# First weight unit of an MLP split ahead of its stage, in buffers of its own

## The chip, the core and the metric

One NeuronCore of a Trainium2 chip runs the whole kernel in one launch. The core has TensorE (matrix multiplication; matmul and weight load are told apart), VectorE, ScalarE, GpSimd and SyncE; the last issues DMAs and waits. The metric is the device time of one execution in microseconds (us). Before the change it was 2215.55 us, the median of 3 runs (2215.15 to 2217.57).

## The reference

One encoder block on `x` (512 frames of 2048 values, float32) with a conditioning vector `c`:

```python
mod = (c_act @ w_ada[i] + b_ada[i])[:, None, :]
shift_m, scale_m, gate_m, shift_f, scale_f, gate_f = jnp.split(mod, N_MOD, axis=-1)

h = rmsnorm(x, g_pre_mix[i]) * (1.0 + scale_m) + shift_m
y = token_mixer(h, w_in[i], ..., w_out[i])          # attention and linear attention, output projection
x = x + gate_m * rmsnorm(y, g_post_mix[i])

h = rmsnorm(x, g_pre_mlp[i]) * (1.0 + scale_f) + shift_f
y = squared_relu_mlp(h, w_mlp_in[i], w_mlp_out[i])  # hidden width 8192
x = x + gate_f * rmsnorm(y, g_post_mlp[i])
```

The change lies between the end of `@ w_out` and the first columns of `h @ w_mlp_in`.

## The kernel before

**Split matmuls.** Each float32 operand is kept as two numbers, a rounded high part and the rest as a low part. One product is three matmuls: high by high, low by high and high by low (`split_mm`, lines 804 to 806). Weights arrive in raw form by DMA, ScalarE copies them to the high part (`split_hi`, line 1246), and VectorE subtracts that from the raw weights for the low part (`split_lo`, line 1716).

**Weight units.** The output projection and the first MLP read their weights in units of 1 MB (512 rows by 512 columns). There are two raw buffers (`w_raw`), two for the high part (`w_hi`) and two for the low part (`w_lo`), all 8 KB per partition, and unit m uses number m % 2 of each. SyncE loads a unit when the one two before it has been split (`slot_free`, line 520). Both splits of a unit wait until TensorE has used the unit two before it (`w_used`, which counts used units). In the program's count the output projection's units are M_OUT to M_OUT + 15; those of the first MLP start at M_MLP.

**The seam.** The output projection runs in four groups of 512 columns. Behind its last group each row block t of 128 frames is squared and summed (`square_y`), multiplied by its gain (`gain_y`), scaled by a root that GpSimd computes (`y_root`) and added to the residual (`add_y`, for rows 2 and 3 in two halves). The sum is squared again (`square_x1`, row 3 in halves), GpSimd computes the next root (`x1_root`), and `scale_x1` gives the normed rows, which TensorE transposes (`x1_transpose`, line 1080). The transposed tile is modulated, rounded to its high part on ScalarE (`modulated_hi`, line 1548) and its low part is made on VectorE (`piece_lo`, line 2212).

**Pieces.** The first MLP block (512 hidden columns) begins before rows 2 and 3 are ready. Its input is cut into 24 pieces:

```python
PIECES = [(slice(h * HALF, (h + 1) * HALF), k) for h in range(2) for k in range(KT // 2)]
PIECES += [(slice(0, SEQ), k) for k in range(KT // 2, KT)]
```

Pieces 0 to 7 are frames 0 to 255 of the inner tiles k = 0 to 7, pieces 8 to 15 frames 256 to 511 of the same tiles, pieces 16 to 23 all frames of k = 8 to 15. Unit 0 holds the weights of k = 0 to 3, so pieces 0 to 3 and 8 to 11 read it; unit 1 serves pieces 4 to 7 and 12 to 15, unit 2 pieces 16 to 19, unit 3 pieces 20 to 23. Unit 0 counts as used at the end of piece 11. A piece has twelve matmuls (four column tiles of 128, three each), with transpositions for a later piece behind it.

**Orders.** Each engine's order is written out by hand. ScalarE: after the projection's last squares and two squares of x1, the split of unit 0, then pieces with squares between; unit 1 is split between pieces 2 and 3, unit 2 behind piece 13's rounding, unit 3 behind piece 17's. VectorE has the matching order. ScalarE multiplies the first gate load by `c` behind the roundings of pieces 19 and 21. SyncE loads units 0, 1 and 2 of the first MLP, then issues the loads for a row of the second gate (`load_gate`, line 618: two of 1 MB into the buffers `ada0`, line 598, and two rows, lines 621 and 623), then loads unit 3 and the next block's units. The buffers `ada0` lie in a region of 16 KB per partition (`R_AD`) that also holds the items of the first gate (`ag_item`), read for the last time in the projection's second group, and, in the second MLP, two raw buffers.

The program ends on a chain through TensorE; the second MLP follows the first without a pause.

Of the kernel before, what the change touches and what calls it, by code (L numbers as in the profile page):

```python
# [45 lines left out]
def build_block(nc, x, c, w_ada, b_ada, g_pre_mix, g_post_mix, w_in, b_fgate, w_gla_a2, b_gla_a2,  # L46
# [67 lines left out]
    with ExitStack() as ctx:  # L114
# [27 lines left out]
        o_junk = at("o_junk", [P, 4, 512], R_A + 8 * KIB)  # L142
        y_t1 = at("y_t1", [P, 2, 4, 512], R_A + 16 * KIB)
        y_t2 = at("y_t2", [P, 2, 4, 512], R_A + 32 * KIB)
        RAW2_AT = (R_C + 32 * KIB, R_C + 40 * KIB, R_AD, R_AD + 8 * KIB, R_A + 56 * KIB)
        v_raw = [at(f"v_raw{s}", [P, 2, 1024], RAW2_AT[s]) for s in range(5)]
        v_op = [at(f"v_op{s}", [P, 2, 1024], R_C + 8 * KIB * s, F32R) for s in range(4)]
        w_raw = [at(f"w_raw{s}", [P, 2048], R_C + 8 * KIB * s) for s in range(2)]
        w_hi = [at(f"w_hi{s}", [P, 2048], R_C + 8 * KIB * (2 + s), F32R) for s in range(2)]
        w_lo = [at(f"w_lo{s}", [P, 2048], R_C + 8 * KIB * (4 + s), F32R) for s in range(2)]  # L150
        grp = at("grp", [P, TILES, SEQ], R_G)
        y = at("y", [P, TB, D], R_G)

# [243 lines left out]

        def arrived_out(cg, mm):
            return RAW_OUT + 16 * (cg * (MM_O // 2) + mm // 2 + 1)

        def arrived_mlp(b, mm):
            return RAW_MLP + 16 * (b * (MM_O // 2) + mm // 2 + 1)
# [116 lines left out]
        def _(sp):  # L519
# [203 lines left out]
            for b in range(FBS):  # L723
                for mm in range(MM_O):
                    load_m1(b, mm)
                    if b % 2 == 0 and mm == 2:
                        load_gate(Q_GF + b // 2, b // 2, GATE_F, g_post_mlp)
                    if b and mm == MM_O - 1 and b - 1 < FBS - 2:
                        store_hidden(b - 1)
# [71 lines left out]
        def _(pe):  # L801
# [331 lines left out]

            def first_mlp_in():
                for n, (cols, k) in enumerate(PIECES):
                    s, m = (k // 4) % 2, M_MLP + k // 4
                    hi, lo = wide_view(w_hi[s])[:, k % 4, :], wide_view(w_lo[s])[:, k % 4, :]
                    if k % 4 == 0:
                        pe.wait_ge(hi_done, m + 1)
                        pe.wait_ge(lo_done, m + 1)  # L1140
                    pe.wait_ge(mod_lo, KT + n + 1)
                    for t in range(4):
                        last = split_mm(bank[t][:, cols], (hi[:, t * P:t * P + P], lo[:, t * P:t * P + P]),
                                        (in_hi[:, k, cols], in_lo[:, k, cols]), k == 0 and n == 0, n == SECOND - 1 or k == KT - 1,
                                        onto=n >= SECOND)
                        if k == KT - 1 and t < 3:
                            last.then_inc(h_sum, 1)
                        if n >= SECOND and t == 3 and k % 4 == 3:
                            last.then_inc(w_used, 1)
                    for following in TRANSPOSES_AT.get(n, ()):  # L1150
                        x1_transpose(following)

            def mlp_in(b):
                steps = [(k, t) for k in range(KT) for t in range(4)]
                if b == LAST:
                    steps = steps[:12 * 4] + [(k, t) for t in range(4) for k in range(12, KT)]
                for k, t in steps:
                    s, m = (k // 4) % 2, M_MLP + b * MM_O + k // 4
                    hi, lo = wide_view(w_hi[s])[:, k % 4, :], wide_view(w_lo[s])[:, k % 4, :]
                    if t == 0 and k % 4 == 0:  # L1160
                        pe.wait_ge(hi_done, m + 1)
                        pe.wait_ge(lo_done, m + 1)
                    if k == 0:
                        if b >= 2:
                            pe.wait_ge(h_relu, 4 * (b - 2) + t + 1)
                        if b == 1:
                            pe.wait_ge(mod_tmp, KT + N_PIECES)
                        if b and b % 2 == 0 and t == 3:
                            pe.wait_ge(ada_col, Q_GF + b // 2)
                    last = split_mm(bank[4 * (b % 2) + t][:, :], (hi[:, t * P:t * P + P], lo[:, t * P:t * P + P]),  # L1170
                                    (in_hi[:, k, :], in_lo[:, k, :]), k == 0, k == KT - 1)
                    if k == KT - 1 and t < 3:
                        last.then_inc(h_sum, 1)
                    if t == 3 and k % 4 == 3:
                        last.then_inc(w_used, 1)
                    if b % 2 and k == KT - 2 and t == 0 and b < LAST or b == LAST and k == KT - 5 and t == 0:

                        pe.wait_ge(h_relu, 4 * b)
                        ada_rows(Q_GF + b // 2, bank[3])
# [61 lines left out]
        def _(act):  # L1241
            def split_hi(m, arrived, n, view=whole_view):
# [2 lines left out]
                act.wait_ge(w_used, m - 1)  # L1245
                act.activation(view(w_hi[n]), view(w_raw[n]), ACT.Copy).then_inc(hi_done, 1)  # L1246


            def next_hi_group(r, mm, last, view):

# [277 lines left out]
            for cg in range(CG):  # L1528
                if cg:
                    for mm in range(2, MM_O):  # L1530
                        split_hi_out(cg * MM_O + mm)
                if cg < CG - 1:
                    split_hi_out(cg * MM_O + MM_O)
                    for t in range(TB):
                        square_y(cg, t)
                    split_hi_out(cg * MM_O + MM_O + 1)
# [18 lines left out]
            square_y(CG - 1, 1)  # L1555
            square_x1(0, 1)
            square_x1(1, 2)
            split_hi_out(CG * MM_O)
            square_y(CG - 1, 2)
            first_piece(0)  # L1560
            square_y(CG - 1, TB - 1)
            first_piece(1)
            first_piece(2)
            split_hi_out(CG * MM_O + 1)
            first_piece(3)
            first_piece(4)
            square_x1(2, 4)
# [7 lines left out]
            for n in range(SECOND, N_PIECES):  # L1575
                if n == N_SECOND:
                    modulate_first(n)
                modulated_hi(n)
                if n in (13, 17):
                    split_hi_out(CG * MM_O + (n - 5) // 4)  # L1580
                if n in (19, 21):
                    ada_times_c(Q_GF, n // 21)
            act.wait_ge(x1_out, 16 * TB)

            def hidden(b):
# [11 lines left out]
                    if b == LAST:  # L1597
                        square_hidden(b, t)
                if b < LAST:
                    split_hi(M_MLP + b * MM_O + 5, arrived_mlp(b + 1, 1), 1)  # L1600
                    for t in range(4):
                        square_hidden(b, t)
                act.wait_ge(h_sq, 4 * b + 4)
# [15 lines left out]
            for b in range(FBS):  # L1619
                for mm in range(MM_O if b == 0 else 0, MM_O):  # L1620
                    if mm != 1:
                        split_hi(M_MLP + b * MM_O + mm, arrived_mlp(b, mm), mm % 2)
                    if mm == 0:
                        hidden(b - 1)
                    if b % 2 == 0 and mm >= 2:
                        ada_times_c(Q_GF + b // 2, mm - 2)
# [84 lines left out]
        def _(dve):  # L1711
            def split_lo(m, n, view=whole_view):
# [3 lines left out]
                dve.tensor_tensor(view(w_lo[n]), view(w_raw[n]), view(w_hi[n]).bitcast(F32), ALU.subtract)\  # L1716
                    .then_inc(lo_done, 1)


            def evict_fox(r, tiles):  # L1720
                for b in tiles:
# [459 lines left out]
            for cg in range(CG):  # L2181
                if cg:
                    for mm in range(2, MM_O):
                        split_lo(M_OUT + cg * MM_O + mm, mm % 2)
                        if cg == 1:
                            for i in (2 * mm - 4, 2 * mm - 3):
                                g_item(GLA_HEADS - 1, i, 0)
                                g_item(GLA_HEADS - 1, i, 1)
                if cg < CG - 1:
                    split_lo(M_OUT + cg * MM_O + MM_O, 0)  # L2190
                    if cg == 1:
# [28 lines left out]
                add_y(t, ALL)  # L2220
            scale_x1(0)
            scale_x1(1)
            split_lo(M_MLP, 0)
            piece_lo(0)
            total_y(2)
            gain_y(CG - 1, 2)
            piece_lo(1)
            total_y(TB - 1)
            gain_y(CG - 1, TB - 1)
            add_y(2, LEFT)  # L2230
            piece_lo(2)
            add_y(2, RIGHT)
            piece_lo(3)
            split_lo(M_MLP + 1, 1)
            piece_lo(4)
            add_y(TB - 1, LEFT)
            add_y(TB - 1, RIGHT)
            piece_lo(5)
            scale_x1(2)
            dve.wait_ge(x1_ss, TB + 1)  # L2240
            dve.tensor_reduce(ss_x[:, TB + 1:TB + 2], ss_x[:, TB - 1:TB + 1], AX_X, ALU.add).then_inc(x1_sq, 1)
# [8 lines left out]
                                  ALU.mult, ALU.add).then_inc(mod_tmp, 1)  # L2250

            modulate_piece(SECOND)
            for n in range(SECOND + 1, N_SECOND):
                modulate_piece(n)
                piece_lo(n - 1)
            piece_lo(N_SECOND - 1)
            split_lo(M_MLP + 2, 0)
            piece_lo(N_SECOND)
            modulate_piece(N_SECOND + 1)
            for n in range(N_SECOND + 2, N_PIECES):  # L2260
                modulate_piece(n)
                piece_lo(n - 1)
                if n == N_SECOND + 2:
                    split_lo(M_MLP + 3, 1)
            piece_lo(N_PIECES - 1)

            def hidden(b):
# [20 lines left out]

            for b in range(FBS):
                for mm in range(MM_O if b == 0 else 0, MM_O):  # L2290
                    split_lo(M_MLP + b * MM_O + mm, mm % 2)
                    if mm == 0 and b and b % 2 == 0:
                        gate_row(Q_GF + b // 2 - 1, b // 2 - 1, bank[3])
                    if mm == 1:
# [305 lines left out]
```

## Time and profile before

| | before |
|---|---|
| median of 3 runs | 2215.55 us (2215.15 to 2217.57) |
| profiled execution | 2217.99 us |
| its span in the profile | 2216.2 us |
| mean granted TensorE clock | 0.997 of full speed |
| TensorE busy, matmul | 2172.1 us, 98% |
| TensorE busy, weight loads | 1757.9 us, 79% |
| VectorE busy | 1531.2 us, 69% |
| ScalarE busy | 880.5 us, 40% |
| GpSimd busy | 375.7 us, 17% |
| DMA | 445.38 MB, mean 201 GB/s |

The rows come from one profiled execution; times in them are us from the start of its span. A row of a timeline gives start, duration, engine, line, operation, what it writes and reads, and in brackets how long the engine sat idle just before it and which engine and line ended that wait. PE is TensorE, PEld its weight loads, DVE VectorE, ACT ScalarE, POOL GpSimd; SPq is SyncE issuing a DMA. Busy shares are averages over stages with different limits, so a stage is read from its own rows.

### The profile page before, as it was taken

Reading aid. Unit: us, or ns where it says so; the run is one execution under the profiler, and the core shown is the slowest. Engines: PE = TensorE matmul, PEld = TensorE weight load, DVE = VectorE, ACT = ScalarE, POOL = GpSimd, SP = SyncE. Lnnn points to the kernel's source line nnn. Section 1 sums busy time; section 2 is a strip of 40 time slices with the busy share of each in tenths; the row PEclk is TensorE's granted clock in tenths of the full one; section 3 lists DMA queues with packets and bytes.
Section 4 is the critical chain, followed back from the end, with each engine's and each line's share of the span. In section 5 each row is a group of like instructions: output and inputs, shape, how many; then the busy total and the mean of one; then the engine's idle time right before and its main releaser. Section 6 shows DMA issues by size and latency. Waiting matters only on the chain.

```text
span 2216.2 us, 26692 instructions
## 1 busy us (share of the span) xinstructions
PE 2172.1 (98%) x9825; PEld 1757.9 (79%) x9825; DVE 1531.2 (69%) x1573; ACT 880.5 (40%) x1126; POOL 375.7 (17%) x208
## 2 busy tenths in 40 slices
PE   6999999999999999999999999999999999999998
PEld 3687888787777887888888888888888888888886
DVE  6987667677776635654465345444689898898998
ACT  5343333332343224533443344335444434444443
POOL 1000000000000001000000000000035455453645
PEclk9999999999999999999999999999999999999999
DMA  9966657553554344474675666646374765577663
GB/s 362 345 218 222 206 169 238 195 162 115 177 169 143 133 171 133 174 253 162 204 237 195 204 203 220 221 168 205 117 231 156 243 224 186 176 243 244 233 233 147
DMA packets 258212, 445.38 MB, mean 201 GB/s; under 512 B 18156, under 2 KB 102320, under 8 KB 252088
## 3 DMA queue, kind: packets, MB, share of 16 engines
q1 hardware_dynamic: 257280, 439.65, 59.1%
q10 hardware_dynamic: 824, 4.27, 0.5%
q8 instruction: 71, 1.16, 0.2%
q14 instruction: 37, 0.30, 0.0%
HBM read 384.08 MB, written 59.79 MB: 200 GB/s over the span
## 4 chain that ended last, share of the span: by engine, by line
PE 83%; issue 8%; DVE 3%; DMA 2%; ACT 1%; DVEq 1%; SPq 1%; POOL 0%; POOLq 0%; ACTq 0%
PE pair L804 26%; PE pair L806 26%; PE pair L805 26%; PE pair L1013 1%; DMA w_raw<-in_w_in 1%; PE pair L902 1%; PE pair L876 1%; PE pair L1024 1%; DMA x_raw<-in_x 1%; DVE v_op L2304 0%; PE pair L893 0%; PE pair L942 0%; DVE w_lo L1716 0%; DVE grp L1915 0%; ACT xn_t L1385 0%
## 5 line engine op out<-in xcount | busy, mean ns | idle before, releaser
L804 PE MATMUL pair<-in_hi,w_hi 128*128 128x512 f32 (+1 forms) x1760 | 703.7, 400 | 7.7 <-DVE in_lo L2212 3.8
L806 PE MATMUL pair<-in_hi,w_lo 128*128 128x512 f32 (+1 forms) x1760 | 681.2, 387 | 0.0
L805 PE MATMUL pair<-in_lo,w_hi 128*128 128x512 f32 (+1 forms) x1760 | 680.2, 386 | 0.0
L1716 DVE TENSOR_TENSOR w_lo<-w_raw,w_hi 128x2048 fp32r<-128x2048 f32 (+2 forms) x142 | 286.4, 2017 | 384.6 <-ACT w_hi L1246 384.2
L1246 ACT ACTIVATE w_hi<-w_raw 128x2048 fp32r<-128x2048 f32 (+2 forms) x142 | 238.5, 1679 | 441.8 <-PE pair L806 413.3
L804 PEld LDWEIGHTS pair<-in_hi,w_hi 128*128 128x128 f32 x1760 | 331.4, 188 | 84.9 <-issue 18.3
L806 PEld LDWEIGHTS pair<-in_hi,w_lo 128*128 128x128 f32 x1760 | 331.1, 188 | 68.7
L805 PEld LDWEIGHTS pair<-in_lo,w_hi 128*128 128x128 f32 x1760 | 331.8, 189 | 65.8 <-issue 2.6
L804 PE MATMUL pair<-v_op,hid_r 128*128 128x512 f32 x896 | 349.0, 390 | 2.1 <-issue 0.9
L806 PE MATMUL pair<-v_op,hid_r 128*128 128x512 f32 x896 | 348.6, 389 | 0.0
L805 PE MATMUL pair<-v_op,hid_r 128*128 128x512 f32 x896 | 348.6, 389 | 0.0
L2304 DVE TENSOR_TENSOR v_op<-v_raw,v_op 128x1024 fp32r<-128x1024 f32 x192 | 302.3, 1595 | 65.1 <-ACT v_op L1689 63.9
L1689 ACT ACTIVATE v_op<-v_raw 128x1024 fp32r<-128x1024 f32 x192 | 203.3, 1061 | 287.4 <-PE pair L806 269.0
L2549 POOL TENSOR_TENSOR v_sum<-v_raw,v_raw 128x512 f32<-128x512 f32 x60 | 149.2, 2513 | 364.2 <-DVE v_raw L2319 364.2
L804 PEld LDWEIGHTS pair<-v_op,hid_r 128*128 128x128 f32 x896 | 168.2, 188 | 38.9 <-issue 3.2
L806 PEld LDWEIGHTS pair<-v_op,hid_r 128*128 128x128 f32 x896 | 168.2, 188 | 35.1
L805 PEld LDWEIGHTS pair<-v_op,hid_r 128*128 128x128 f32 x896 | 168.2, 188 | 34.6
L2558 POOL TENSOR_TENSOR v_raw<-v_raw,v_sum 128x512 f32<-128x512 f32 x60 | 135.3, 2285 | 18.4 <-DVE v_op L2304 18.4
L2475 POOL TENSOR_TENSOR ada<-ada,c_act 128x2048 f32<-128x2048 f32 x8 | 30.9, 3864 | 591.1 <-DMA ada<-in_w_ada 553.9
L2354 DVE TENSOR_TENSOR y_t<-pair,y_t 128x1024 f32<-128x1024 f32 x104 | 125.0, 1215 | 0.3 <-PE pair L806 0.3
L804 PE MATMUL pair<-w_hi,in_hi 128*128 128x512 f32 x256 | 101.2, 395 | 0.0
L805 PE MATMUL pair<-w_lo,in_hi 128*128 128x512 f32 x256 | 99.7, 389 | 0.0
(240 smaller groups left out, 2037.0 us busy)
## 6 DMA issues: line engine op xcount, KB each, us to landing
w_raw<-in_w_mlp_in SPq DMA_DIRECT2D x64, 1024.0 KB, 5.3
v_raw<-in_w_mlp_out SPq DMA_DIRECT2D x128, 512.0 KB, 5.0
hid_r<-hid_scratch SPq DMA_DIRECT2D x112, 512.0 KB, 6.4
hid_scratch<-hid_r SPq DMA_DIRECT2D x28, 1792.0 KB, 6.6
am_item<-in_w_ada SPq DMA_DIRECT2D x64, 512.0 KB, 8.7
af_item<-in_w_ada SPq DMA_DIRECT2D x64, 512.0 KB, 4.7
w_raw<-in_w_in SPq DMA_DIRECT2D x96, 256.0 KB, 3.8
w_raw<-in_w_in SPq DMA_DIRECT2D x160, 128.0 KB, 3.7
```

The lines of the kernel that those rows point to most:

```text
L804: pe.matmul(dst, a[0], b[0], start=start, stop=False, skip_group_check=onto)
L805: pe.matmul(dst, a[0], b[1], start=False, stop=False, skip_group_check=onto)
L806: return pe.matmul(dst, a[1], b[0], start=False, stop=stop, skip_group_check=onto)
L876: pe.matmul(BA[:, 0:(i + 1) * P], grp[:, q_tile, i * P:i * P + P], grp[:, k_tile, 0:(i + 1) * P], start=True, stop=True).then_inc(fox_qk, 1)
L1246: act.activation(view(w_hi[n]), view(w_raw[n]), ACT.Copy).then_inc(hi_done, 1)
L1689: act.activation(v_op[i % 4][:, 0, :], raw_of(u, p)[:, h, :], ACT.Copy).then_inc(v_hi, 1)
L1716: dve.tensor_tensor(view(w_lo[n]), view(w_raw[n]), view(w_hi[n]).bitcast(F32), ALU.subtract)\
L2304: dve.tensor_tensor(v_op[i % 4][:, 1, :], raw_of(u, p)[:, h, :], v_op[i % 4][:, 0, :].bitcast(F32), ALU.subtract).then_inc(v_lo, 1)
L2354: return dve.tensor_tensor(dst, src[:, :, :], dst, ALU.add)
L2475: pool.tensor_tensor(unit[:, :, :], unit[:, :, :], c_act[:, :].rearrange("p (k o) -> p k o", o=1).to_broadcast([P, KT, P]), ALU.mult)\
L2549: last = pool.tensor_tensor(v_sum[:, h, cols], v_raw[q[B22]][:, h, cols], v_raw[q[B11]][:, h, cols], ALU.add)
L2558: last = pool.tensor_tensor(b21, b21, v_sum[:, h, cols], ALU.subtract)
```

## The change

Weight unit 0 of the first MLP gets buffers of its own for its high and low part, `m1_hi[0]` and `m1_lo[0]` in the region `R_AD`. It is split at the end of the output projection's last group, behind that group's last unit, on ScalarE and on VectorE. The later units use the two old pairs, chosen by `m1_slot(j)`: even units number 1, odd units number 0. Unit 1 is split where unit 0 was on ScalarE, and where it was before on VectorE. Because the region also takes the first gate row's loads, SyncE waits, behind the load of unit 2, until unit 0 has been used. In VectorE's order at the seam four places change: `piece_lo(1)` moves behind `gain_y` of row 3, `piece_lo(5)` ahead of the second half of `add_y` of row 3, `piece_lo(8)` ahead of `modulate_piece(9)`, and unit 0's low split leaves. The second MLP's raw and operand buffers exchange places so that they match the units that come free last.

```diff
         y_t2 = at("y_t2", [P, 2, 4, 512], R_A + 32 * KIB)
-        RAW2_AT = (R_C + 32 * KIB, R_C + 40 * KIB, R_AD, R_AD + 8 * KIB, R_A + 56 * KIB)
+        RAW2_AT = (R_C + 40 * KIB, R_C + 32 * KIB, R_AD, R_AD + 8 * KIB, R_A + 56 * KIB)
         v_raw = [at(f"v_raw{s}", [P, 2, 1024], RAW2_AT[s]) for s in range(5)]
-        v_op = [at(f"v_op{s}", [P, 2, 1024], R_C + 8 * KIB * s, F32R) for s in range(4)]
+        v_op = [at(f"v_op{s}", [P, 2, 1024], R_C + 8 * KIB * (0, 1, 3, 2)[s], F32R) for s in range(4)]
...
         w_lo = [at(f"w_lo{s}", [P, 2048], R_C + 8 * KIB * (4 + s), F32R) for s in range(2)]
+        m1_hi = [at("m1_hi", [P, 2048], R_AD, F32R), *w_hi]
+        m1_lo = [at("m1_lo", [P, 2048], R_AD + 8 * KIB, F32R), *w_lo]
...
+        def m1_slot(j):
+            return 2 - j % 2 if j else 0
...
                     load_m1(b, mm)
+                    if b == 0 and mm == 2:
+                        sp.wait_ge(w_used, M_MLP + 1)
...
                 for n, (cols, k) in enumerate(PIECES):
-                    s, m = (k // 4) % 2, M_MLP + k // 4
-                    hi, lo = wide_view(w_hi[s])[:, k % 4, :], wide_view(w_lo[s])[:, k % 4, :]
+                    s, m = m1_slot(k // 4), M_MLP + k // 4
+                    hi, lo = wide_view(m1_hi[s])[:, k % 4, :], wide_view(m1_lo[s])[:, k % 4, :]
...
                 for k, t in steps:
-                    s, m = (k // 4) % 2, M_MLP + b * MM_O + k // 4
-                    hi, lo = wide_view(w_hi[s])[:, k % 4, :], wide_view(w_lo[s])[:, k % 4, :]
+                    s, m = m1_slot(b * MM_O + k // 4), M_MLP + b * MM_O + k // 4
+                    hi, lo = wide_view(m1_hi[s])[:, k % 4, :], wide_view(m1_lo[s])[:, k % 4, :]
...
+            def split_hi_mlp(j):
+                act.wait_ge(w_in_s[j % 2], arrived_mlp(j // MM_O, j % MM_O))
+                if j == 0:
+                    act.wait_ge(am_used, G_USED + GLA_HEADS * G_ITEMS)
+                else:
+                    act.wait_ge(w_used, M_MLP + j - (1 if j > 2 else 2))
+                act.activation(m1_hi[m1_slot(j)][:, :], w_raw[j % 2][:, :], ACT.Copy).then_inc(hi_done, 1)
...
                         split_hi_out(cg * MM_O + mm)
+                if cg == CG - 1:
+                    split_hi_mlp(0)
...
             square_x1(1, 2)
-            split_hi_out(CG * MM_O)
+            split_hi_mlp(1)
...
             first_piece(2)
-            split_hi_out(CG * MM_O + 1)
...
                 if n in (13, 17):
-                    split_hi_out(CG * MM_O + (n - 5) // 4)
+                    split_hi_mlp((n - 5) // 4)
...
                 if b < LAST:
-                    split_hi(M_MLP + b * MM_O + 5, arrived_mlp(b + 1, 1), 1)
+                    split_hi_mlp(b * MM_O + 5)
...
                     if mm != 1:
-                        split_hi(M_MLP + b * MM_O + mm, arrived_mlp(b, mm), mm % 2)
+                        split_hi_mlp(b * MM_O + mm)
...
+            def split_lo_mlp(j):
+                dve.wait_ge(hi_done, M_MLP + j + 1)
+                if j:
+                    dve.wait_ge(w_used, M_MLP + j - (1 if j > 2 else 2))
+                dve.tensor_tensor(m1_lo[m1_slot(j)][:, :], w_raw[j % 2][:, :], m1_hi[m1_slot(j)][:, :].bitcast(F32),
+                                  ALU.subtract).then_inc(lo_done, 1)
...
                                 g_item(GLA_HEADS - 1, i, 1)
+                if cg == CG - 1:
+                    split_lo_mlp(0)
...
             scale_x1(1)
-            split_lo(M_MLP, 0)
...
             gain_y(CG - 1, 2)
-            piece_lo(1)
...
             gain_y(CG - 1, TB - 1)
+            piece_lo(1)
...
             piece_lo(3)
-            split_lo(M_MLP + 1, 1)
+            split_lo_mlp(1)
...
             add_y(TB - 1, LEFT)
+            piece_lo(5)
             add_y(TB - 1, RIGHT)
-            piece_lo(5)
...
             modulate_piece(SECOND)
-            for n in range(SECOND + 1, N_SECOND):
+            piece_lo(SECOND)
+            modulate_piece(SECOND + 1)
+            for n in range(SECOND + 2, N_SECOND):
...
             piece_lo(N_SECOND - 1)
-            split_lo(M_MLP + 2, 0)
+            split_lo_mlp(2)
...
                 if n == N_SECOND + 2:
-                    split_lo(M_MLP + 3, 1)
+                    split_lo_mlp(3)
...
                 for mm in range(MM_O if b == 0 else 0, MM_O):
-                    split_lo(M_MLP + b * MM_O + mm, mm % 2)
+                    split_lo_mlp(b * MM_O + mm)
```

## Rows read from the trace of the kernel before

**Rows 1.** The page, busy us of each engine, share of the span, instructions.

```profile
PE 2172.1 (98%) x9825; PEld 1757.9 (79%) x9825; DVE 1531.2 (69%) x1573; ACT 880.5 (40%) x1126; POOL 375.7 (17%) x208
```

**Rows 2.** Waits of TensorE, whole span: who waited for whom, us, times, longest.

```profile
PE pair L804 <- DVE in_lo L2212: 3.8, 7, 0.8
```

**Rows 3.** TensorE's timeline: first matmul of pieces 6, 8, 17, 18; last of 11.

```profile
885.73 0.39 PE L804 MATMUL pair<-in_hi,w_hi 128*128 128x256 f32 x1 [0.51 <-DVE in_lo L2212]
...
891.11 0.36 PE L804 MATMUL pair<-in_hi,w_hi 128*128 128x256 f32 x1 [0.84 <-DVE in_lo L2212]
...
897.43 0.28 PE L806 MATMUL pair<-in_hi,w_lo 128*128 128x256 f32 x1
...
908.14 0.48 PE L804 MATMUL pair<-in_hi,w_hi 128*128 128x512 f32 x1
...
911.35 0.48 PE L804 MATMUL pair<-in_hi,w_hi 128*128 128x512 f32 x1
```

**Rows 4.** ScalarE's timeline: unit 0's split, a square, piece 6, unit 3's split.

```profile
867.01 1.91 ACT L1246 ACTIVATE w_hi<-w_raw 128x2048 fp32r<-128x2048 f32 x1
...
883.16 1.06 ACT L1525 ACTIVATE y<-x_res 128x1024 f32<-128x1024 f32 x1
...
884.22 0.55 ACT L1542 ACTIVATE in_tmp<-pair,mod_b,mod_a 128x256 f32<-128x256 f32 x1
...
905.18 1.90 ACT L1246 ACTIVATE w_hi<-w_raw 128x2048 fp32r<-128x2048 f32 x1
```

**Rows 5.** VectorE's timeline: row 3's additions, pieces 9 and 8, from unit 3's split.

```profile
880.65 2.47 DVE L2206 SCALAR_TENSOR_TENSOR x_res<-y,rstd,x_res 128x1024 f32<-128x1024 f32 x2
...
890.09 0.54 DVE L2249 TENSOR_SCALAR in_tmp<-pair,mod_a,mod_b 128x256 f32<-128x256 f32 x1 [1.21 <-PE pair L1080]
890.55 0.41 DVE L2212 TENSOR_TENSOR in_lo<-in_tmp,in_hi 128x256 fp32r<-128x256 f32 x1
...
907.12 2.29 DVE L1716 TENSOR_TENSOR w_lo<-w_raw,w_hi 128x2048 fp32r<-128x2048 f32 x1 [0.48 <-ACT w_hi L1246]
909.33 0.81 DVE L2249 TENSOR_SCALAR in_tmp<-pair,mod_a,mod_b 128x512 f32<-128x512 f32 x1
910.05 0.68 DVE L2212 TENSOR_TENSOR in_lo<-in_tmp,in_hi 128x512 fp32r<-128x512 f32 x1
```

**Rows 6.** SyncE's DMA issues: gate loads and unit 3, first block; same, third block.

```profile
872.10 4.91 SPq L598 DMA_DIRECT2D ada<-in_w_ada  x2
...
881.58 0.38 SPq L565 DMA_DIRECT2D w_raw<-in_w_mlp_in  x1
...
967.29 4.93 SPq L598 DMA_DIRECT2D ada<-in_w_ada  x2
...
978.66 0.38 SPq L565 DMA_DIRECT2D w_raw<-in_w_mlp_in  x1
```

**Rows 7.** DMAs issued 871.68, 872.10, 881.58, 978.66, us to landing; GB/s, 40 slices of 820-960.

```profile
w_raw<-in_w_mlp_in SPq DMA_DIRECT2D x1, 1024.0 KB, 5.6
ada<-in_w_ada SPq DMA_DIRECT2D x1, 1024.0 KB, 8.8
...
w_raw<-in_w_mlp_in SPq DMA_DIRECT2D x1, 1024.0 KB, 7.4
...
w_raw<-in_w_mlp_in SPq DMA_DIRECT2D x1, 1024.0 KB, 5.2
...
GB/s 106 198 0 19 281 0 43 256 0 28 272 8 0 0 0 276 313 291 321 435 428 403 16 0 271 52 277 5 0 0 0 95 221 286 356 430 280 284 2 258
```

**Rows 8.** A wait of TensorE, and two stretches: busy us by engine, PEclk, DMA share, GB/s.

```profile
677.52 0.47 PE L804 MATMUL pair<-in_hi,w_hi 128*128 128x512 f32 x1 [1.83 <-DVE w_lo L1716]
...
676.00:680.00 4.00, 2.48 (x8) 2.00 (x9) 3.32 (x4) 1.69 (x1) 0.00 (x0) 0.79 0.32 68
680.00:682.00 2.00, 2.00 (x6) 1.19 (x4) 0.00 (x0) 0.00 (x0) 0.00 (x0) 0.56 1.05 410
```

## The prediction

> **What bounds the kernel now.** I read the busy shares first: TensorE is busy for 98% of the span [rows 1], so only the stretches where it stands still, or something that makes it stand still, can move the time. Then the waits of TensorE over the whole span: of its waits on VectorE for a piece of the MLP's input (line 2212) there are 7, and they sum to 3.8 us, the longest 0.8 us [rows 2]. All lie in the stretch that the change touches, from the end of the output projection to piece 8 of the first MLP unit. Last the timelines of that stretch, engine by engine [rows 3 to 6]. The reader is to see there that TensorE gets pieces 0 to 8 late, and that from piece 8 at 891.11 to the end of the MLP's first block it runs without a stop: piece 17 starts at 908.14, piece 18 at 911.35, with no idle time in their rows [rows 3]. Time won before piece 8 therefore stays won, unless something later is late. That something is in the queue of SyncE.
>
> **Part 1, unit 0's split moved into the output projection.** Both halves of weight unit 0 are made in buffers of their own while the projection's last group still runs, where both engines idle for several us at a time between splits. They leave the stretch. One ScalarE split of 1.9 us goes (unit 1 takes the place of unit 0 at 867.01 [rows 4]), and one VectorE split of 2.3 us, by the row of another [rows 5]. I cost the split at nothing in its new place: its data is issued for as soon as out unit 14 is split, and 1.9 + 2.3 us fit into an idle stretch.
>
> What it wins is less than it removes, because the chain to each piece is not VectorE's alone. Piece 6 shows it. Before, its start at 885.73 [rows 3] followed from the second half-row square at 883.16 (1.06 us), then ScalarE's modulation at 884.22 (0.55 us) [rows 4] and its two roundings. That square waits for the two additions of row 3, which ended at 880.65 + 2.47 = 883.12 [rows 5]. In the new order the second of these two additions stands behind `piece_lo(5)`, which waits for ScalarE's piece 5, itself behind the square of row 2. Following each instruction with its duration of before, I get the addition's end at 882.85 instead of 883.12: piece 6 wins 0.3 us. Bounds: 0 (the addition is no earlier), and 1.9 us (the whole ScalarE split). I take 0.3, since squares, modulation and rounding stay behind it.
>
> Piece 8 waited 0.84 us more [rows 3], because its `piece_lo` (890.55) stood behind `modulate_piece(9)`, which had waited 1.21 us for its transposition [rows 5]. The change puts `piece_lo(8)` ahead. Bounds 0 and 1.2 us; I take 0.9, the wait itself. Sum at piece 8: 0.3 + 0.9 = 1.2 us won, between 0 and 3.1.
>
> **Part 2, a wait added in SyncE's queue.** The own buffers of unit 0 are the memory of the gate-row items, so SyncE now waits, behind the load of unit 2, until unit 0 is used up. In the order of the pieces that is the end of piece 11, since pieces 0 to 3 and 8 to 11 read unit 0. Queued behind the wait are two gate loads of 1 MB, two small rows, **and the load of weight unit 3** (then those of the next block). Before, the first gate load was issued at 872.10 and unit 3's at 881.58 [rows 6]. Who waits for unit 3: ScalarE, which splits it right behind piece 17's rounding and has piece 18's rounding queued behind it, and VectorE likewise.
>
> Step by step:
> - Piece 11's last matmul ran at 897.43 for 0.28 us [rows 3], so 897.71; minus the 1.2 us won, 896.5. SyncE issues 0.1 us later, 896.6.
> - From the first gate issue to the landing of unit 3. Before: 881.58 + 7.4 - 872.10 = 16.9 us. In the block of 967 us: 978.66 + 5.2 - 967.29 = 16.6 us [rows 6, 7]. Both had another weight load of 1 MB just ahead of them in the queue, which the new place has not. The first gate load behind that weight load landed 8.8 us after its issue; a 1 MB load with nothing ahead takes 5.2 to 5.6 [rows 7]; the difference, 3.2 us at the least, falls away. 16.6 - 3.2 = **13.4 us**. Unit 3 lands at 910.0.
> - ScalarE splits it (1.90 us [rows 4]), VectorE makes the low half (2.29), modulates piece 19 (0.81) and only then makes piece 18's low half (0.68) [rows 5]: with the small overlaps that these rows have, 5.7 us, and 0.1 for each of two hand-overs. Piece 18 starts at 896.6 + 13.4 + 5.9 = 915.9, that is 4.5 us later than before.
> - TensorE would have been ready at 911.35 - 1.2 = 910.15, so it stands for 5.7 us. What the clock does to that: a wait of 1.83 us at 677.52 was followed by a fall to the lower level, 1.2 GHz. The granted clock is 0.79 over 676 to 680 and 0.56 over 680 to 682 [rows 8], which is (0.21 x 4 + 0.44 x 2) / 0.5 = 3.4 us at half speed, or 1.7 us of work lost. A wait three times as long I expect to cost the same **1.7 us**; bounds 0 and 3.4 (one such stretch more).
> - From piece 18 on each piece has its inputs before TensorE comes to it, and TensorE is the bound of all that follows, so nothing is given back.
>
> Bounds of the 13.4 us: 16.9 us above (as in the row of before, weight load included). Below, 3 MB of loads and 0.3 MB of rows at the highest rate of any slice, 435 GB/s [rows 7], are 7.8 us, and 2.1 us from issue to the first data (5.6 less the 3.5 us that 1 MB takes at some 300 GB/s): 9.9 us.
>
> The Trainium skill, page "DMA: Bandwidth & Descriptors", section "Bandwidth", has HBM at some 358 GB/s for a core as the limit of such loads. The slices of this trace lie at 276 to 321 GB/s while the gate loads run and above that only while stores run beside them [rows 7]. By the page's figure each MB would take 0.6 us less, and as an estimate the sum would come out about 1.8 us lower, still slower than before.
>
> **Part 3, the other buffers.** Units 1, 2, 3, ... use the other one of two pairs, and the second MLP's buffers are exchanged to fit. The waits they stand behind are for the same units as before, so 0. ScalarE's split of unit 2 no longer waits for piece 11, which was 0.5 us of its idle time and not on the path: TensorE ran.
>
> **Sum.** 4.5 + 1.7 = +6.2 us. The profiled execution took 2217.99 us (span 2216.2 and 1.8 around it), so 2224.2 for it; it was 2.4 us above the median of the runs. On the median: 2215.55 + 6.2 = **2221.7 us**.
>
> **Rivals.**
> - *Faster: the load of unit 3 is not late.* If SyncE's issues go through at once and unit 3 lands within 910.15 - 5.9 - 896.6 = 7.7 us of the first gate issue, TensorE never stands at piece 18 and the 1.2 us stay: 2214.4. Against it: 3.3 MB in 7.7 us is more than any slice shows. It decides at 7.7 us, and the lower bound is 9.9. Chance 4%.
> - *Slower by less: the queue drains at the highest rate.* 9.9 us in place of 13.4, so piece 18 is 1.0 us late and the standing, 2.2 us, is short enough that the clock may hold: +1.0 to +2.7, 2217.4. For it: nothing but these loads runs then. Against: the slices with gate loads alone lie at 276 to 321 GB/s. Chance 16%.
> - *The clock holds at piece 18.* The rest as forecast: +4.5, 2220.1. Against it is the fall after 1.83 us. Chance 8%.
> - *The new order wins nothing.* Pieces 2 to 5 come up to 1.9 us earlier but piece 6 only 0.3, so the wait ahead of piece 6 grows from 0.51 to some 2.1 us, longer than the one after which the clock fell. If it falls there, the 1.2 us are gone: +7.4, 2222.9. Chance 20%.
> - *The queue is as slow as before and the clock falls twice.* 16.9 us in place of 13.4: 7.4 + 3.5 = +10.9, 2226.4. Chance 8%.
>
> **How the numbers follow.** The forecast itself has 44%. Two tenths of a per cent, 4.4 us, is about what a measurement of this kernel tells from no change. Faster by more than that is out of reach of every case but a chain that I have missed, 0.03. Within it: the faster rival, the fast queue, the held clock in part, and the low edge of the forecast: 0.27. Slower: the rest, 0.70. The range takes in the fast queue below and the slow one above: 2216.5 to 2226.5.
>
> **What would show it.** In the changed profile TensorE's chain should name a wait ahead of piece 18, at about 910, of 4 to 7 us, released by VectorE's low half. ScalarE's split of unit 3 should sit idle before it, released by the DMA of the weights. SyncE's first gate load should be issued at about 896.6, unit 3's about 7 to 9 us later. The granted clock should fall near 914. The seven waits of line 2212 should shift to one large one ahead of piece 6. Wrong it is if unit 3 lands before 905, if piece 18 starts by 911, or if TensorE's start at piece 8 is more than 3 us earlier.

## The result and the profile after

The changed kernel took 2224.38 us, the median of 6 runs (2223.38 to 2227.05), against 2215.74 us for the kernel before (6 runs): a ratio of 1.0037, 95% interval 1.0027 to 1.0047. The forecast was slower, 2221.7 us, with a range of 2216.5 to 2226.5.

The busy shares are the same to the per cent: 98% of TensorE, as before [rows 1]. What changed is seen in TensorE's waits. Of the changed kernel, whole span:

```profile
PE pair L811 <- DVE in_lo L2237: 8.9, 4, 5.9
```

Seven waits that summed to 3.8 us [rows 2] have become four that sum to 8.9, and one of them is 5.9 us long. TensorE's timeline shows which. First the projection's last matmul and the first of the second MLP block in the kernel before:

```profile
871.17 0.40 PE L806 MATMUL pair<-w_hi,in_lo 128*128 128x512 f32 x1
...
929.54 0.47 PE L804 MATMUL pair<-in_hi,w_hi 128*128 128x512 f32 x1
```

Then the changed kernel: the projection's last matmul, the first of pieces 6 and 8, the last of piece 11, the first of pieces 17, 18 and 19, and the first of the second block.

```profile
870.70 0.40 PE L813 MATMUL pair<-w_hi,in_lo 128*128 128x512 f32 x1
...
884.92 0.39 PE L811 MATMUL pair<-in_hi,w_hi 128*128 128x256 f32 x1 [2.05 <-DVE in_lo L2237]
...
889.98 0.36 PE L811 MATMUL pair<-in_hi,m_hi 128*128 128x256 f32 x1
...
896.33 0.29 PE L813 MATMUL pair<-in_hi,m_lo 128*128 128x256 f32 x1
...
907.04 0.48 PE L811 MATMUL pair<-in_hi,w_hi 128*128 128x512 f32 x1
...
916.42 0.79 PE L811 MATMUL pair<-in_hi,w_hi 128*128 128x512 f32 x1 [5.94 <-DVE in_lo L2237]
...
921.09 0.48 PE L811 MATMUL pair<-in_hi,w_hi 128*128 128x512 f32 x1
...
936.08 0.47 PE L811 MATMUL pair<-in_hi,w_hi 128*128 128x512 f32 x1
```

The stretch from the projection's last matmul to the second block was 58.37 us and is 65.38: **+7.0 us**. I call it S below. It leaves out what happens elsewhere in an execution, so it tells apart steps of under 1 us, which whole times do not. Counted from the projection's last matmul, piece 8 comes 0.66 us earlier (19.28 against 19.94) and piece 18 comes 5.5 us later (45.72 against 40.18; the 0.66 us won are in this already). From piece 18 to the second block another 1.5 us is lost (19.66 against 18.19), and 5.5 + 1.5 = 7.0.

Who released piece 18 is read from ScalarE and SyncE, in the changed kernel:

```profile
910.82 1.91 ACT L1262 ACTIVATE w_hi<-w_raw 128x2048 fp32r<-128x2048 f32 x1 [6.66 <-DMA w_raw<-in_w_mlp_in]
```

```profile
896.64 2.71 SPq L603 DMA_DIRECT2D ada<-in_w_ada  x2
...
903.86 0.38 SPq L570 DMA_DIRECT2D w_raw<-in_w_mlp_in  x1
```

Before, that split ran at 905.18 without a wait [rows 4]. Now ScalarE stands 6.66 us for the weights, whose load SyncE issued at 903.86 and not at 881.58 [rows 6]. The times from issue to landing of the first gate load and of unit 3, and the GB/s of 885 to 925 in slices of 1 us:

```profile
ada<-in_w_ada SPq DMA_DIRECT2D x1, 1024.0 KB, 6.6
...
w_raw<-in_w_mlp_in SPq DMA_DIRECT2D x1, 1024.0 KB, 6.9
...
GB/s 131 393 401 467 434 401 393 442 434 426 270 0 67 211 309 326 311 291 289 292 288 274 311 375 395 408 258 76 0 0 0 143 313 406 186 0 0 0 0 16
```

And VectorE behind it, three steps of the sum in one view (unit 3's low half, piece 19's modulation, piece 18's low half):

```profile
912.76 2.29 DVE L1740 TENSOR_TENSOR w_lo<-w_raw,w_hi 128x2048 fp32r<-128x2048 f32 x1 [7.22 <-ACT w_hi L1262]
914.97 0.80 DVE L2273 TENSOR_SCALAR in_tmp<-pair,mod_a,mod_b 128x512 f32<-128x512 f32 x1
915.69 0.68 DVE L2237 TENSOR_TENSOR in_lo<-in_tmp,in_hi 128x512 fp32r<-128x512 f32 x1
```

The granted clock (the column after POOL) over piece 6 and over the standing:

```profile
885.00:887.00 2.00, 2.00 (x11) 2.00 (x12) 1.40 (x2) 0.31 (x1) 0.00 (x0) 0.61 0.63 262
887.00:889.00 2.00, 2.00 (x12) 2.00 (x11) 0.61 (x2) 0.42 (x1) 0.00 (x0) 0.54 1.06 434
...
912.00:914.00 2.00, 0.00 (x0) 0.00 (x0) 1.24 (x1) 1.25 (x2) 0.00 (x0) 0.69 0.10 38
914.00:916.00 2.00, 0.00 (x0) 0.00 (x0) 2.00 (x3) 0.20 (x1) 0.00 (x0) 0.50 0.00 0
916.00:918.00 2.00, 1.58 (x4) 1.29 (x5) 1.69 (x3) 2.00 (x7) 0.00 (x0) 0.50 0.90 228
918.00:920.00 2.00, 2.00 (x7) 1.57 (x6) 0.00 (x0) 1.29 (x4) 0.00 (x0) 0.61 0.76 296
```

It fell twice: behind the wait of 2.05 us ahead of piece 6, and during the one of 5.94 us, so that piece 18 began at 1.2 GHz. The second fall is some 3.7 us ahead of piece 18 (0.69 over 912 to 914 means 1.2 GHz from about 912.8; 0.61 over 918 to 920, until about 919.6), so more than half of that low stretch passed while TensorE stood anyway.

### The profile page after: what moved, and what is told of

Read it like the earlier page. It is cut to its first block, busy times and chain, and to the rows that moved or that the text cites. A ratio compares the mean times of both kernels' runs of the same rounds, so it can differ in the third digit from the quotient of the medians.

```text
span 2222.6 us, 26692 instructions
## 1 busy us (share of the span) xinstructions
PE 2174.6 (98%) x9825; PEld 1760.5 (79%) x9825; DVE 1531.2 (69%) x1573; ACT 880.6 (40%) x1126; POOL 373.3 (17%) x208
## 4 chain that ended last, share of the span: by engine, by line
PE 90%; DVE 3%; DMA 2%; ACT 2%; DVEq 1%; issue 1%; SPq 1%; POOLq 0%; POOL 0%; ACTq 0%
PE pair L811 28%; PE pair L813 28%; PE pair L812 28%; PE pair L1020 1%; DMA w_raw<-in_w_in 1%; PE pair L909 1%; PE pair L1031 1%; PE pair L883 1%; DMA x_raw<-in_x 1%; DVE v_op L2330 0%; PE pair L900 0%; DVE w_lo L1732 0%; PE pair L949 0%; DMA w_raw<-in_w_mlp_in 0%; DVE grp L1938 0%
## 5 line engine op out<-in xcount | busy, mean ns | idle before, releaser
L811 PE MATMUL pair<-in_hi,w_hi 128*128 128x512 f32 (+1 forms) x1728 | 694.8, 402 | 12.6 <-DVE in_lo L2237 8.7
L813 PE MATMUL pair<-in_hi,w_lo 128*128 128x512 f32 (+1 forms) x1728 | 672.7, 389 | 0.0
L812 PE MATMUL pair<-in_lo,w_hi 128*128 128x512 f32 (+1 forms) x1728 | 671.9, 389 | 0.0
L811 PEld LDWEIGHTS pair<-in_hi,w_hi 128*128 128x128 f32 x1728 | 326.0, 189 | 88.6 <-issue 16.1
L813 PEld LDWEIGHTS pair<-in_hi,w_lo 128*128 128x128 f32 x1728 | 325.8, 189 | 68.7
L812 PEld LDWEIGHTS pair<-in_lo,w_hi 128*128 128x128 f32 x1728 | 326.4, 189 | 65.8 <-issue 2.6
L1740 DVE TENSOR_TENSOR w_lo<-w_raw,w_hi 128x2048 fp32r<-128x2048 f32 x63 | 146.9, 2332 | 302.4 <-ACT w_hi L1262 302.4
L1262 ACT ACTIVATE w_hi<-w_raw 128x2048 fp32r<-128x2048 f32 x63 | 120.5, 1912 | 238.1 <-PE pair L813 231.5
L1732 DVE TENSOR_TENSOR w_lo<-w_raw,w_hi 128x1536 fp32r<-128x1536 f32 (+2 forms) x78 | 137.2, 1758 | 88.0 <-ACT w_hi L1253 87.6
L1253 ACT ACTIVATE w_hi<-w_raw 128x1536 fp32r<-128x1536 f32 (+2 forms) x78 | 116.0, 1488 | 202.4 <-PE pair L813 175.0
```

Of the source, the lines that this page charges most:

```text
L811: pe.matmul(dst, a[0], b[0], start=start, stop=False, skip_group_check=onto)
L812: pe.matmul(dst, a[0], b[1], start=False, stop=False, skip_group_check=onto)
L813: return pe.matmul(dst, a[1], b[0], start=False, stop=stop, skip_group_check=onto)
L1262: act.activation(m1_hi[m1_slot(j)][:, :], w_raw[j % 2][:, :], ACT.Copy).then_inc(hi_done, 1)
L1740: dve.tensor_tensor(m1_lo[m1_slot(j)][:, :], w_raw[j % 2][:, :], m1_hi[m1_slot(j)][:, :].bitcast(F32), ALU.subtract).then_inc(lo_done, 1)
```

## The experiments

Three theories. A: unit 3's load stands behind the wait and the gate loads, and piece 18 waits for it. B: the new order at the seam, with the clock's fall at piece 6, costs the time. C: the early split delays the projection. Ratios are to the kernel before, run beside them on the same chip, with 95% intervals. Beside the first four kernels (unit 3 ahead of the wait, the wait alone, the standing filled, row 3 first) the kernel before had a median of 2217.68 us (27 runs), beside the other four 2216.83 us (23 runs). So whole times of the two sets are compared by their ratios.

| kernel | ratio | piece 8 | piece 18 | S | S less before |
|---|---|---|---|---|---|
| before | 1 | 19.94 | 40.18 | 58.37 | 0 |
| changed | 1.0037 (1.0027 to 1.0047) | 19.28 | 45.72 | 65.38 | +7.0 |
| changed, again | 1.0026 (1.0015 to 1.0038) | 19.26 | 46.03 | 67.01 | +8.6 |
| unit 3 ahead of the wait | 0.9990 (0.9981 to 0.9999) | 19.27 | 39.54 | 57.75 | -0.6 |
| wait alone | 1.0035 (1.0021 to 1.0049) | 19.92 | 47.00 | 67.82 | +9.4 |
| wait, unit 3, gate loads | 1.0004 (0.9995 to 1.0013) | 19.28 | 39.53 | 57.74 | -0.6 |
| standing filled | 1.0020 (1.0011 to 1.0029) | 19.27 | 46.18 | 64.39 | +6.0 |
| row 3 first | 0.9987 (0.9977 to 0.9996) | 17.79 | 38.05 | 56.24 | -2.1 |
| unit 1 split early | 0.9995 (0.9986 to 1.0004) | 17.83 | 38.07 | 56.27 | -2.1 |
| piece 8 alone | one run | 18.83 | 39.09 | 57.29 | -1.1 |

Pieces and S are us from the projection's last matmul, each from one profile. Two kernels with the same S (57.75 and 57.74) have ratios of 0.9990 and 1.0004, so a difference of 0.001 between two ratios is not read here as an effect of an edit.

**Unit 3 ahead of the wait** (changed kernel).

```diff
-                    if b == 0 and mm == 2:
+                    if b == 0 and mm == 3:
                         sp.wait_ge(w_used, M_MLP + 1)
-                    if b % 2 == 0 and mm == 2:
+                    if b % 2 == 0 and mm == (2 if b else 3):
                         load_gate(Q_GF + b // 2, b // 2, GATE_F, g_post_mlp)
```

> The changed kernel with one thing moved: SyncE loads weight unit 3 ahead of the new wait and the gate loads, everything else stays. Theory A (unit 3 arrives late because its load stands behind the wait and the gate loads): the wait ahead of piece 18 is gone, ScalarE's split of unit 3 has no idle time before it, and what is left is the 0.6 to 1.2 us that the new order won before piece 8: 2214 to 2215.5 us, that is 0 to -1.5 against before and 7 to 10 us under the changed kernel. Theory B (the seam's new order and the clock's fall at piece 6 cost the time, the late load is mostly hidden): it stays at 2220 or more. Theory C (the split in the projection's last group delays its end): TensorE's last projection matmul would come later against the start of that group than in the kernel before, and the time stays above 2218.

2215.06 us (11 runs), ratio 0.9990. Its waits for pieces, piece 18 (no idle time in the row), and ScalarE's split of unit 3 (none either):

```profile
PE pair L811 <- DVE in_lo L2237: 3.0, 3, 2.1
```

```profile
907.83 0.48 PE L811 MATMUL pair<-in_hi,w_hi 128*128 128x512 f32 x1
```

```profile
901.66 1.90 ACT L1262 ACTIVATE w_hi<-w_raw 128x2048 fp32r<-128x2048 f32 x1
```

All of the slowdown is gone with unit 3's load moved forward in SyncE's order: A holds, and B and C fall, since the seam's order and the early split are still in. The traces of the kernel before and the changed one say the same of C: from the first to the last high by high matmul of the projection's last group it takes 43.5 us in both.

**The wait alone** (kernel before).

```diff
                     load_m1(b, mm)
+                    if b == 0 and mm == 2:
+                        sp.wait_ge(w_used, M_MLP + 1)
```

> The kernel before with one thing added: SyncE's wait until unit 0 is used, ahead of the gate loads; no buffers, no new order (the wait is not needed for the data there). Theory A: the whole slowdown appears, and a little more, since nothing is won before piece 8: the first gate load at 897.8, unit 3 lands 14.2 us later as in the changed kernel at 912.0, piece 18 starts at 917.9 instead of 911.35 (+6.5), the clock falls once or twice in the 6.6 us of standing (+1.5 to 1.7): +8 us, 2223 to 2225.5. Theory B: no more than 3 us above before.

2225.57 us (5 runs), ratio 1.0035, just above the 2223 to 2225.5 that I expected. Piece 18 and ScalarE's split:

```profile
916.35 0.79 PE L806 MATMUL pair<-in_hi,w_hi 128*128 128x512 f32 x1 [6.58 <-DVE in_lo L2214]
```

```profile
910.74 1.91 ACT L1248 ACTIVATE w_hi<-w_raw 128x2048 fp32r<-128x2048 f32 x1 [7.30 <-DMA w_raw<-in_w_mlp_in]
```

The wait brings the whole loss without the rest of the change: piece 18 is 6.8 us late (6.5 expected). S is 9.4 us longer, because the clock stayed low for longer than expected: from piece 18 to the second block it takes 20.82 us in place of 18.19, so 2.6 us are lost.

```profile
914.00:916.00 2.00, 0.00 (x0) 0.00 (x0) 2.00 (x3) 0.27 (x1) 0.00 (x0) 0.50 0.00 0
916.00:920.00 4.00, 3.65 (x9) 2.88 (x10) 1.62 (x3) 3.22 (x10) 0.00 (x0) 0.50 0.81 262
920.00:922.00 2.00, 2.00 (x7) 1.51 (x6) 0.00 (x0) 0.00 (x0) 0.00 (x0) 0.50 0.00 0
```

**Wait, then unit 3, then the gate loads** (changed kernel).

```diff
+                    if b == 0 and mm == 3:
+                        sp.wait_ge(w_used, M_MLP + 1)
                     load_m1(b, mm)
-                    if b == 0 and mm == 2:
-                        sp.wait_ge(w_used, M_MLP + 1)
-                    if b % 2 == 0 and mm == 2:
+                    if b % 2 == 0 and mm == (2 if b else 3):
```

> The changed kernel with SyncE's order behind the wait turned round: unit 3's load first, then the gate loads. So unit 3 stands behind the wait as in the changed kernel, but not behind the gate loads. If the wait by itself makes it late, piece 18 still stands for 4 to 6 us. By my sum it is the gate loads in front: a weight load alone lands 5.2 to 5.6 us after its issue, piece 18 is not held up below 7.7 us, so no wait ahead of piece 18, and the time equals that of the kernel with unit 3 ahead of the wait: 0 to -1.5 us against before, 0.9990 within 0.001.

2217.0 us (11 runs), ratio 1.0004, above what I expected of the whole time; S is 57.74, the same as with unit 3 ahead of the wait, as expected. SyncE's issue of unit 3:

```profile
894.45 0.37 SPq L570 DMA_DIRECT2D w_raw<-in_w_mlp_in  x1
```

It landed 5.7 us later, and ScalarE split it at 901.87 with no idle time. So the wait by itself costs nothing in this stretch; what is late is a load behind 2 MB of gate loads. Why this ratio is 0.0014 above that of the kernel with unit 3 ahead of the wait, with the same S, stays open.

**The standing filled** (changed kernel; the 24 added products are read by nobody).

```diff
+                    if n == N_SECOND + 2:
+                        pe.wait_ge(mod_tmp, KT + n + 1)
+                        for _ in range(24):
+                            pe.matmul(bank[4 + n % 4][:, :], hi[:, 0:P], in_hi[:, KT // 2, :], start=True, stop=True)
                     pe.wait_ge(mod_lo, KT + n + 1)
```

> The changed kernel with 24 matmuls of 512 columns (their sum is read by nobody) in TensorE's standing time ahead of piece 18: 24 x 0.227 = 5.4 us of the 5.9 us idle there, so the clock should hold at 1.00 through piece 18. If the clock's fall costs what the rows say (piece 20 is 6.5 us late where piece 18 was 5.1 late, so 1.5 us), the time is 1.5 us under the changed kernel, 2222 to 2223.5, and piece 18 still starts when unit 3 lets it. If the lost 1.5 us are something else (a wait behind piece 18), the time is that of the changed kernel.

2221.41 us (11 runs), ratio 1.0020, somewhat below the 2222 to 2223.5 that I expected. The clock through the filled time and piece 18:

```profile
910.00:914.00 4.00, 3.22 (x15) 2.33 (x13) 3.52 (x3) 1.43 (x3) 0.00 (x0) 1.00 0.05 13
914.00:918.00 4.00, 3.85 (x19) 3.21 (x20) 1.77 (x4) 3.02 (x10) 0.00 (x0) 1.00 0.82 261
```

```profile
914.15 0.50 PE L811 MATMUL pair<-in_hi,w_hi 128*128 128x512 f32 x1 [0.93 <-DVE in_lo L2241]
```

From piece 18 to the second block it takes 64.39 - 46.18 = 18.21 us, as before (18.19). So the 1.5 us lost behind piece 18 in the changed kernel are the clock, and nothing else waits there. Piece 18 itself is as late as in the changed kernel (46.18 us against 45.72 and 46.03).

**Row 3's addition first** (on top of unit 3 ahead of the wait).

```diff
             add_y(TB - 1, LEFT)
-            piece_lo(5)
             add_y(TB - 1, RIGHT)
+            piece_lo(5)
```

> The first kernel of this set (unit 3 loaded ahead of the wait) with one more step undone: the second half of row 3's addition stands ahead of piece 5's low half again, as before the change. My step for piece 6 says that this addition, held up by piece 5, is what eats the gain: it should end at about 881.6 instead of 882.3, piece 6 starts 0.7 us earlier and piece 5 0.9 us later, the wait ahead of piece 6 falls from 2.05 us to under 1, and the clock no longer falls there: 0.7 to 1.4 us under the first kernel, about 2213.5. If the order does not matter (the square of row 2 sets it), it equals the first kernel within 0.5 us.

2213.66 us (11 runs), ratio 0.9987: below the kernel before, by 2.1 us of S. Pieces 5 and 6, and the clock:

```profile
880.29 0.39 PE L811 MATMUL pair<-in_hi,w_hi 128*128 128x256 f32 x1 [0.75 <-DVE in_lo L2237]
882.51 0.39 PE L811 MATMUL pair<-in_hi,w_hi 128*128 128x256 f32 x1 [0.53 <-DVE in_lo L2237]
```

```profile
880.00:884.00 4.00, 3.18 (x24) 2.98 (x24) 2.78 (x5) 2.83 (x7) 1.58 (x3) 1.00 0.63 242
884.00:888.00 4.00, 3.54 (x30) 3.30 (x30) 2.92 (x7) 0.94 (x3) 0.00 (x0) 1.00 1.01 418
```

Piece 6 starts 13.50 us after the projection in place of 14.20, as expected, the one wait of 2.05 us is two short ones of 1.28 us together, and the clock holds. From piece 6 to piece 8 it takes 4.29 us, where it took 5.07 with the clock's fall; in the 4.29 is a wait of 0.46 us ahead of a transposition, which the slower matmuls had covered. S is 1.5 us shorter than with unit 3 ahead of the wait alone: 0.7 us of it come before piece 6, and 0.8 us, net of that wait, from the clock. That is 0.1 more than the most I expected.

**Piece 8 alone** (kernel before, one run).

```diff
             modulate_piece(SECOND)
-            for n in range(SECOND + 1, N_SECOND):
+            piece_lo(SECOND)
+            modulate_piece(SECOND + 1)
+            for n in range(SECOND + 2, N_SECOND):
```

> The kernel before with one step of the change done alone: piece 8's low half ahead of the modulation of piece 9 on VectorE. By my step piece 8 wins its wait of 0.84 us and the start behind it, 0.9 to 1.1 us from the projection's last matmul to piece 8 (19.94 us before, so 18.9 to 19.0), and everything behind it moves by the same. If another chain (ScalarE's rounding, TensorE's transposition) is as late, it wins under 0.3.

Piece 8 comes at 18.83 us: 1.1 us are won, and S is shorter by the same 1.1. The single run, 2217.21 us, is no basis for a ratio.

**Unit 1 split early** (on top of row 3 first).

```diff
             scale_x1(1)
+            split_lo_mlp(1)
             piece_lo(0)
...
             piece_lo(3)
-            split_lo_mlp(1)
```

> The kernel with row 3's addition ahead of piece 5 and unit 3 loaded ahead of the wait, with one step more: unit 1's low split on VectorE stands ahead of piece 0's low half, where VectorE sat idle for 1.6 us, in place of ahead of piece 4's. Piece 0 starts up to 0.6 us later, the wait ahead of piece 4 (0.66 us) goes, row 3's additions end about 2 us earlier, and piece 8 comes 1 to 2 us earlier than in that kernel (17.8 us from the projection's last matmul, so 16 to 17). Time: 1 to 2 us under it, 0.998 of before. If the root of row 2 or row 3 on GpSimd sets pieces 6 and 7 instead, it wins under 0.5.

2215.73 us (11 runs), ratio 0.9995, and piece 8 at 17.83: nothing won, my expectation missed. The wait ahead of piece 4 went, but piece 0 starts 0.45 us later, piece 5 still waits (0.81 us, 0.75 without this step), piece 6 waits longer (1.29 in place of 0.53), and piece 8 now waits 0.41 us. Pieces 5 and 6:

```profile
883.87 0.38 PE L811 MATMUL pair<-in_hi,w_hi 128*128 128x256 f32 x1 [0.81 <-DVE in_lo L2237]
886.85 0.39 PE L811 MATMUL pair<-in_hi,w_hi 128*128 128x256 f32 x1 [1.29 <-DVE in_lo L2237]
```

VectorE itself sat idle for 1.40 us ahead of piece 4's low half, for ScalarE's rounding, which had waited for TensorE's transposition behind piece 2. So at that piece VectorE's order is not the bound. That it is no bound of pieces 5 to 8 either is not shown.

**The changed kernel again.**

> The changed kernel, unaltered, beside the others of this call. Its ratio to before was 1.0037; with the same stretches as before I expect 1.003 to 1.0045 again, the standing ahead of piece 18 between 5.5 and 6.5 us, and the sum of granted-clock stretches at the lower level to differ from run to run.

2222.78 us (7 runs), ratio 1.0026, just under what I expected; the standing is 6.26 us, and 20.98 us go from piece 18 to the second block, so the clock cost 2.8 us here against 1.5 in the first profile.

## Why the prediction was right, point by point

- *What bounds.* Right: what was won before piece 8 stayed (pieces 8 to 17 keep their 0.6 us), and the late load took more.
- *Part 1, 1.2 us at piece 8.* Nearly twice too high: 0.66 us was measured. Piece 6 won 0.34 us (14.22 against 14.56), as worked out (0.3). Piece 8's step is worth 1.1 us when done alone (0.9 taken). But the clock fell behind the wait ahead of piece 6 and took 0.8 us net back (0.34 + 1.1 - 0.8 = 0.64). I had that as a rival with a chance of 20%, at 2222.9 us, so the case that came is nearer to this rival than to the forecast's own, though 0.66 us of the gain stayed. The clock fell there in all five profiles that have the wait of 2 us, and in none of the five others, where piece 6 waited 0.5 to 1.3 us.
- *Part 2, where and when.* Right: SyncE's wait holds the gate loads and unit 3 back, the split waits for the DMA of the weights, piece 18 waits for VectorE's low half. That the gate loads were issued at 896.64, with 896.6 forecast, is luck: piece 8 was 0.5 us later than I took, and the projection ended 0.5 us earlier in this profile (870.70 against 871.17).
- *From issue to landing, 13.4 us.* Too low: 903.86 + 6.9 - 896.64 = 14.1. The mis-sized term is what falls away with no weight load in front: 16.6 - 14.1 = 2.5 us, where I took 3.2. I had it from a gate load's 8.8 us less the 5.6 of a weight load, but a gate load with nothing ahead took 6.6 us. By parts it is another sum. From the first gate load's issue to that of unit 3 it took 7.2 us, where the block of 967 us took 11.4, so 4.2 us fell away. From unit 3's issue to its landing it took 6.9 us and not that block's 5.2, so 1.7 us came back. The load of unit 4, the next block's first, was issued 0.5 us behind unit 3's here, and no load followed that closely in the block of 967 us; whether this made the landing longer is not shown. The slices with gate loads lie at 274 to 326 GB/s here, those of 908 to 911, when only weight loads were left, at 375 to 408. The Trainium skill's figure ("DMA: Bandwidth & Descriptors", "Bandwidth", 358 GB/s) would have made the sum shorter; the measured rates lie below it with gate loads and above it without, so it is no limit in this trace.
- *Piece 18, +4.5.* 5.5 measured: 0.5 more from the smaller gain, 0.7 more from the landing, 0.2 less from there to piece 18 (916.42 - 910.76 = 5.7, where I had 5.9).
- *The clock, 1.7.* 1.5, 2.6 and 2.8 us in three profiles with this standing, 0 when it was filled: inside the bounds of 0 and 3.4, and on average above what I took. That the first profile is so near to 1.7 is partly luck: I took a low stretch that lies on work only, and here more than half of it lay on the standing.
- *Part 3 and the split's new place at nothing.* No new wait of TensorE stands in the projection's last group, which takes 43.5 us as before, and S is shorter than before without the late load.
- *Sum.* +6.2 forecast; S grew by 7.0 and 8.6 us in the two profiles, the medians by 8.6 us in the first comparison and by 6.0 in the second (2222.78 against 2216.83).

## What to carry to other kernels

A wait put into a queue delays everything issued behind it (unit 3's load was issued at 903.86 and not at 881.58): list what stands there before pricing it, loads of other stages too, and put what is needed soonest ahead. Turning that order round here took a loss of 0.37% back to the time of the kernel before (ratios of 0.9990 and 1.0004, S 0.6 us shorter). Where work leaves an engine, look at which wait then becomes one long one: here one wait of 2.05 us was followed by the clock's fall, which cost 0.8 us more, and two waits of 0.75 and 0.53 us were not.

## What the runs showed of the hardware

The input projection (`@ w_in`) has, near its end, a wait of TensorE of 1.82 to 1.84 us in all ten profiles (677.52 in the kernel before [rows 8]). It was followed by the fall to 1.2 GHz in some of them and not in others. In the changed kernel the clock held:

```profile
678.65 0.47 PE L811 MATMUL pair<-in_hi,w_hi 128*128 128x512 f32 x1 [1.82 <-DVE w_lo L1732]
```

```profile
678.00:680.00 2.00, 1.35 (x6) 1.16 (x7) 1.91 (x4) 0.84 (x1) 0.00 (x0) 1.00 0.12 14
680.00:682.00 2.00, 2.00 (x9) 1.31 (x8) 0.69 (x2) 0.00 (x0) 0.00 (x0) 1.00 0.90 308
```

With row 3 first it was 0.50 over 677 to 679, behind 1.83 us at 675.39; over the ten profiles it fell there in five. In the kernel before such a fall is worth 1.7 us of work. It is in the profile of the kernel before and not in the first of the changed kernel, so their whole times differ by only 6.4 us (2224.42 less 2217.99) where S differs by 7.0. How much of the spread of one kernel's whole times such falls make up is not shown: the runs without a profile show only the mean clock.
